# Input projection of a hybrid decoder step, from plain float32 products to three products of rounded parts and rests, with GpSimd making the rests

## The reference, cut to what matters

```
xn = rmsnorm(h, norm1_g)
proj = xn @ w_in + b_in                      # 2048 -> 4096
c_val, c_gate, l_x, l_gate = split(proj)     # 1024 each
u = c_val * sigmoid(c_gate)
c = silu(layernorm(causal_dw_conv(u, width 31)))
lx = causal_dw_conv(l_x, width 4)
r, i = sigmoid(lx @ w_a + b_a), sigmoid(lx @ w_x + b_x)   # per head of 128
log_a = -8 * r * softplus(-lam);  a = exp(log_a)
h_t = a_t * h_{t-1} + sqrt(-expm1(2 log_a)) * i * lx      # over time
h = h + concat(c, hs * gelu(l_gate)) @ w_out
```

## Time and profile before

| what | value |
|---|---|
| median of 3 runs | 1488.46 us (1486.98 to 1491.21) |
| the profiled execution's own time | 1490.41 us |
| its span, first to last instruction | 1488.7 us |
| PE busy | 1383.9 us (93%) |
| DVE busy | 608.9 us (41%) |
| ACT busy | 229.1 us (15%) |
| POOL busy | 40.8 us (3%) |
| mean granted TensorE clock | 0.985 |

### The profile page before, as it was taken

How to read it: one execution, slowest core, us unless ns; L and a number is a source line. 1 busy time by engine, 2 the same in 40 slices (tenths; PEclk the granted TensorE clock), 3 DMA queues, 4 the chain that set the end, 5 groups by cost and what they waited for, 6 DMA issues and landing times.

```text
span 1488.7 us, 19036 instructions
## 1 busy us (share of the span) xinstructions
PE 1383.9 (93%) x7574; PEld 806.0 (54%) x7574; DVE 608.9 (41%) x1030; ACT 229.1 (15%) x369; POOL 40.8 (3%) x56
## 2 busy tenths in 40 slices
PE   8999999999989999999999999989999998997995
PEld 7888888899753333333333333333333333333995
DVE  5689645544542232232223222322232223225764
ACT  2000147533200000000000000000000000003552
POOL 0000000000000000000000000000000000000000
PEclk9999999999999999999999999999999999998998
DMA  9553342345769999999999999999999999999341
GB/s 381 218 198 125 113 122 86 142 142 198 270 241 382 422 422 422 422 422 422 422 422 422 422 422 422 422 421 422 421 422 422 422 422 421 422 422 401 143 142 59
DMA packets 72523, 486.26 MB, mean 327 GB/s; under 512 B 8416, under 2 KB 12544, under 8 KB 15120
## 3 DMA queue, kind: packets, MB, share of 16 engines
q1 hardware_dynamic: 71040, 482.98, 79.8%
q0 software_dynamic: 320, 1.59, 0.3%
q10 hardware_dynamic: 1120, 1.09, 0.2%
HBM read 481.06 MB, written 5.65 MB: 327 GB/s over the span
## 4 chain that ended last, share of the span: by engine, by line
PE 51%; DMA 40%; DVE 3%; ACT 3%; issue 2%; SPq 1%; DVEq 0%; ACTq 0%
DMA ring<-in_w_up_dram 39%; PE ps L816 14%; PE ps L625 14%; PE ps L838 5%; PE ps L688 4%; PE ps L689 4%; PE ps L690 4%; PE ps L849 2%; DVE hT L1551 1%; DMA embedding_rows<-ple_stage 1%; PE ps L634 1%; SPq L472 1%; PE ps L776 1%; PE ps L777 1%; PE ps L715 1%
## 5 line engine op out<-in xcount | busy, mean ns | idle before, releaser
L816 PE MATMUL ps<-ring,xwin 128*64 128x512 f32 x1984 | 452.6, 597 | 37.5 <-DMA ring<-in_w_up_dram 37.2
L1551 DVE TENSOR_TENSOR hT<-hT,ps 128x1056 f32<-128x1056 f32 x128 | 160.4, 1254 | 373.3 <-PE ps L849 372.3
L816 PEld LDWEIGHTS ps<-ring,xwin 128*64 128x64 f32 x1984 | 150.5, 136 | 292.7 <-issue 292.7
L838 PE MATMUL ps<-ring,hid 128*64 128x512 f32 x1024 | 233.6, 610 | 18.8 <-DVE hid L1531 18.8
L625 PE MATMUL ps<-xT,ring 128*128 128x264 f32 x1024 | 229.7, 386 | 0.0
L625 PEld LDWEIGHTS ps<-xT,ring 128*128 128x128 f32 x1024 | 194.5, 190 | 33.5 <-issue 0.3
L838 PEld LDWEIGHTS ps<-ring,hid 128*64 128x64 f32 x1024 | 74.6, 140 | 154.1 <-issue 152.7
L849 PE MATMUL ps<-S,ysb 64*128 64x264 f32 x1024 | 148.3, 408 | 1.3 <-issue 0.8
L849 PEld LDWEIGHTS ps<-S,ysb 64*128 64x128 f32 x1024 | 88.4, 186 | 110.9 <-issue 102.3
L1096 ACT ACTIVATE sgl<-ps 64x512 f32<-64x512 f32 x32 | 18.8, 588 | 575.4 <-PE ps L816 575.4
L1543 DVE COPY ysb<-ps 128x512 f32<-128x512 f32 x32 | 22.1, 691 | 181.8 <-PE ps L838 181.8
(11 more groups left out here) (271 smaller groups left out, 1021.1 us busy)
## 6 DMA issues: line engine op xcount, KB each, us to landing
ring<-in_w_gate_dram SPq DMA_DIRECT2D x128, 1024.0 KB, 23.4
ring<-in_w_up_dram SPq DMA_DIRECT2D x128, 1024.0 KB, 25.4
ring<-in_w_down_dram SPq DMA_DIRECT2D x128, 1024.0 KB, 24.1
ring<-in_w_in_dram SPq DMA_DIRECT2D x32, 1024.0 KB, 7.9
ring<-in_w_out_dram SPq DMA_DIRECT2D x16, 1024.0 KB, 4.8
ring<-in_w_pg_dram SPq DMA_DIRECT2D x16, 1024.0 KB, 5.1
hT<-in_x_dram SPq DMA_DIRECT2D x4, 528.0 KB, 5.2
pleT<-embedding_rows SPq DMA_DIRECT2D x1, 2112.0 KB, 21.5
```

Of the source, the lines that this page charges most:

```text
L816: mm = pe.matmul(ps[part * WIN:(part + 1) * WIN, 0, :], window(k), weights(2 * j + part)[:, kk * F:(kk + 1) * F], start=(k == 0), stop=(k ...
L838: mm = pe.matmul(ps[half * WIN:(half + 1) * WIN, 2 + b, :], hid[:, t, :], weights(8 + t)[:, q * 512:(q + 1) * 512], start=(t == 0), stop=( ...
L1551: dve.tensor_tensor(group(hT, g), group(hT, g), ps[:, bank:bank + 4, 0:TOK].rearrange("p (h k) t -> p h k t", h=2), ALU.add)\
```

## The change

The input projection is now made as the output projection is: weights and xn are rounded, rests are kept, and three float32r products replace each float32 product. Weights come as whole output tiles (48 tiles `t` in one sequence: 32 of `w_in`, 16 of `w_out`), four low slots and four high slots in turn. ACT rounds tile n+3 after it has taken tile n out of PSUM. POOL makes the rests of the first 35 tiles (32 of `w_in`, 3 of `w_out`); DVE makes the others as before. The convolution sums on DVE go to PSUM bank 5 until the last term. `R` has a second buffer, `I2` and `IR` separate two other uses of `I`, and the pieces of the recurrence stand in a new order on PE, ACT and DVE.

```
-CH_IN = 32
...
+W_IN = 32
+W_OUT = 16
+W_FRONT = W_IN + W_OUT
...
+LRU_AT = 23
...
+POOL_RESTS = W_IN + 3
...
     @block.sync
...
-            sp.dma_start(ring[:, slot(n), :], a["w_in"][n]).then_inc(slot_loaded[slot(n)], 16)
...
+        for t in range(PG_SLOTS, W_FRONT):
+            sp.wait_ge(acc_full, t - PG_SLOTS + 1)
             load_tile(t)
+            if t == W_IN + 3:
+                for k in range(CH_PLE):
+                    sp.dma_start(ring[:, PLE_SLOT + k, PLE_HEAD * P:], a["w_ple"][k, :, PLE_HEAD * P:]).then_inc(ple_loaded, 16)
...
+        def rest_weights(t):
+
+            pool.wait_ge(w_hi_ready, t + 1)
...
+            pool.tensor_tensor(lo, ring[:, lo_slot(t), :], hi.bitcast(F32), ALU.subtract).then_inc(w_lo_ready, 1)
+
+        for t in range(POOL_RESTS):
+            rest_weights(t)
...
-        for n in range(CT_OUT):
-            dense(n, 4 * (n // 4), xT, KD, wait_xT if n == 0 else None)
-            if 20 <= n < 28:
-                lru_gates(n - 20)
-            if n == 23:
...
+        hi_hi(0)
+        lo_hi(0, last=False)
+        hi_hi(1)
+        hi_lo(0, last=True)
+        hi_lo(1)
+        lo_hi(1)
+        for n in range(2, W_IN):
+            if n >= 3:
+                pe.wait_ge(acc_free, n - 3 + 1)
+            hi_hi(n)
+            hi_lo(n)
+            if LRU_AT <= n < LRU_AT + 4:
+                lru_gates(2 * (n - LRU_AT))
+            lo_hi(n)
+            if LRU_AT <= n < LRU_AT + 4:
+                lru_gates(2 * (n - LRU_AT) + 1)
+            if n == 22:
                 mean()
-            if 26 <= n < 30:
-                var(n - 26)
+            if n == 26:
+                var()
...
+        for k in range(KD):
+            act.wait_ge(xT_ready, k + 1)
+            act.activation(x_part(k), xT[:, k, :], ACT.Copy).then_inc(x_hi_ready, 1)
...
+            round_weights(n + 3)
+            if n == 24:
+                betas(0)
...
+        for k in range(KD):
+            dve.wait_ge(x_hi_ready, k + 1)
+            dve.tensor_tensor(x_lo[:, k, :], xT[:, k, :], x_part(k).bitcast(F32), ALU.subtract).then_inc(x_lo_ready, 1)
...
+                    part = ps[:, 5, j % 2 * SEQ:j % 2 * SEQ + SEQ]
...
-                        last[j] = step(stt(mix[:, j, 0:SEQ], U[:, j, t:t + SEQ], w, mix[:, j, 0:SEQ],
+                        last[j] = step(stt(mix[:, j, 0:SEQ] if t == CK - 1 else part, U[:, j, t:t + SEQ], w, part,
```

More of the change, by code:

```diff
@@ L40 @@
 PG_SLOTS = 4
[L41 to L48, removed]
+EXP_SLOT = [8, 0, 9, 1, 10, 2, 11, 3, 4, 5, 6, 7]
+HEAD_SLOT = 4
+MIX_SLOT = 4
+X_SLOT = 6
+PLE_SLOT = 6
+MIX_ORDER = list(range(KD))
+LRU_AT = 23
+TAIL_LO = [8, 9, 10, 11, 4, 6]
+TAIL_HI = [0, 1, 2, 3, 5, 7]
 TAIL_SLOTS = len(TAIL_LO)
@@ L599, in turn, with embed @@
             return pe.matmul(out, src, ident[:, :], start=True, stop=True)
[L601 to L627, removed]
+        def embed(n):
+            pe.wait_ge(ple_taken, n - 3 - CT_PLE + 1) if n - 3 >= CT_PLE else pe.wait_ge(h1_ready, n - 3 - CT_OUT + 1)
+            if n == CT_PLE:
+                pe.wait_ge(ple_loaded, 32)
+            m = PLE_HEAD + n - CT_PLE
+            for k in range(CH_PLE):
+                mm = pe.matmul(ps[:, n % 3, 0:TOK], ring[:, PLE_SLOT + k, m * P:(m + 1) * P], pT[:, k, :],
+                               start=(k == 0), stop=(k == CH_PLE - 1))
             mm.then_inc(acc_full, 1)
         pe.wait_ge(consts_ready, 5)
[L631 to L634, removed]
+        for q in range(XQ):
+            pe.wait_ge(x_summed, q + 1)
+            mm = pe.matmul(ps[:, 0, 0:TOK], ones[:, :], T[:, q, :], start=(q == 0), stop=(q == XQ - 1))
         mm.then_inc(row_full, 1)
@@ L660, in mean, with var @@
             mm.then_inc(mean_full, 1)
-        def var(p):
-            pe.wait_ge(sq_ready, 2 * p + 2)
-            for j in range(2 * p, 2 * p + 2):
-                mm = pe.matmul(ps[:, 7, 0:TOK], ones[:, :], sq[:, j % 2, :], start=(j == 0), stop=(j == TC - 1))
+        def var():
+            pe.wait_ge(sq_ready, 2)
+            for j in range(TC):
+                mm = pe.matmul(ps[:, 7, 0:TOK], ones[:, :], sq[:, j, :], start=(j == 0), stop=(j == TC - 1))
             mm.then_inc(sq_used, 1)
-        def wait_xT(k):
-            pe.wait_ge(xT_ready, k + 1)
@@ new lines, in lo_hi @@
+        def lo_hi(n, last=True):
+            pe.wait_ge(*rest_in(n))
+            for k in range(KD):
+                mm = pe.matmul(ps[:, n % 3, 0:TOK], ring_r[:, lo_slot(n), k, :], x_part(k), start=False,
+                               stop=(last and k == KD - 1))
+            if last:
+                mm.then_inc(acc_full, 1)
+        hi_hi(0)
[15 more added lines that the diff above has]
+            if n == 22:
@@ L1046, in _ @@
                     round_mix(j)
-        act.wait_ge(mixr_ready, TC)
-        round_mix(KD - 1)
-        round_weights(2)
+            if n == 30:
+                for j in range(6):
+                    act.wait_ge(mixr_ready, j + 1)
+                    round_mix(TC + j)
+        for j in (6, 7):
+            act.wait_ge(mixr_ready, j + 1)
+            round_mix(TC + j)
         def square_h1(m):
```

388 lines of the change are left out of this document (208 added, 180 removed).

## The result

The changed kernel takes 1516.12 us in the median of 4 runs (1515.13 to 1517.12), the kernel before 1489.84 in the 4 runs beside them: a ratio of 1.0177, with an interval from 1.0155 to 1.0199. It is slower by 26 us where the forecast had 1470.9 and a range up to 1500. The profiled execution has a span of 1514.8 us against 1488.7 before; the first output tile ("the mark") ends at 296.5 and not at 271.2, 25 us later, so the loss lies ahead of it and is carried nearly unchanged to the end.

The account below looks back on a forecast made before the run. PE was taken to bound the input stage, up to the first output tile's end at 271.2 us. Gain 27.6 less 10 for collisions is 17.6, off 1490.41: 1472.8, or 1470.9 on the median's footing; range 1455 to 1500.

Parts of the forecast that it names:

- Tile 1: Start of the input stage: its end taken at 35.5 us against 33.5 before, a loss of 2 us.
- stall at tile 25: Second pair of gate products in tile 25: PE waits 7 us for PSUM banks that ACT's gates clear.
- that at tile 26: PE waits 2 us more for ACT at tile 26, until 200.5 us.
- Without collisions: End of the first output tile if no DVE instruction meets a POOL subtraction: 243.6 us, a gain of 27.6.
- the step on collisions: Behind tile 22, DVE instructions with two SBUF inputs meet POOL subtractions: 0 to 17 us together, taken as 10.
- four places: Both halves of the second recurrence, the scaling by the deviation, the last rests of mix: 0 to 4.2 us each.
- a collision or so in each group: Convolution on DVE, four groups from 47.7 us: ends at 156 instead of 150, still in time for the mean.
- this sign of being wrong: Listed under what would show the forecast wrong: waits of the mean on the convolution.
- Strict turns: Rival, chance 0.18: whole subtractions alternate with single two-input DVE instructions; gain only 6 us, time 1482.5.
- The other slower rivals: POOL's subtraction as dear as its select, 1509 us, chance 0.09; sums in PSUM exposing their chain, 1496.9, chance 0.06.
- the exposed chain: Rival, chance 0.06: convolution sums in PSUM add 28 us on DVE, 2 find room; time 1496.9.
- POOL at its dearest: Rival, chance 0.09: a POOL subtraction takes 7.95 us like its select; first output tile 21 us slower, time 1509.

Follow-up runs that it names:

- e2_memset: The changed kernel with GpSimd writing zeros instead of subtracting, so the rests of those weights are left out: 1461.5 us in one run.
- e5_conv: The changed kernel with small operations and gates of the convolution freed of second SBUF operands, and state products made by POOL: 1484.8 us.
- e6_tail: The changed kernel with POOL's last six tiles of rests (29 to 34) made by DVE instead: 1497.1 us.
- e1_small: The changed kernel with the kc operations at the start of DVE's program and the spt scratch in PSUM: 1514.0 us.
- e8_nodma: The changed kernel with GpSimd's two DMA issues after its fifth subtraction moved to the SyncE queue: 1516.4 us.

## Why the prediction was wrong, point by point

*Right.* Tile 1 ended at 36.1 (forecast 35.5). The tiles of the input stage follow at 5.83 us (5.84). POOL's subtraction takes 4.7 us (4.2, within its bounds), under the pace of a tile, so PE waited only 3.5 us in six places for rests of weights. The Trainium skill (GPSIMD Engine Reference, Performance versus the Vector engine) gives 4.5 us for a two-input operation of this size; a subtraction undisturbed took 4.50, the mean of 35 with the disturbed ones 4.71. The sums in PSUM cost nothing more. The stall at tile 25 on ACT's gates was 7.5 us (7), that at tile 26 1.4 (2). Without collisions the mark would be at 243.8 (243.6): shown by e2_memset.

*Wrong: the step on collisions.* The prediction wrote "on the chain behind tile 22 four places can meet a subtraction ... each costs 0 to 4.2, together 0 to 17; I take 10". The loss against the mark without collisions is 52.7 us (296.5 less 243.8). It failed in three ways.

First, it looked behind tile 22 only. Ahead of it, it had the convolution start "when tile 3 is out, at 47.7", and gave it "a collision or so in each group". The chain between the rests of x and the first tap, nineteen instructions of DVE of which thirteen are 128x1 or 128x8 and take some 0.2 us each, was not in the working at all. It cost 28 us of start, and 9.3 us more were lost between the third and the fourth group; a slack of 16 us took part of it, and 21.5 us reached the mean. e5_conv gives 31.3 us back when these alone are cured. The prediction had named this sign of being wrong itself: waits of the mean on the convolution.

Second, the tail. Six places and not four met a subtraction (a product of the recurrence, the sum of 128x32, a gate's product, one of the scalings, two rests of mix), and the upper end of one collision was a whole subtraction, right in kind; a gate's product met a subtraction and a DMA issue (6.3 us), and the rests of mix met two in a row (9.2). PE waited 17.3 us there against 2.0 in e2_memset. e6_tail gives 19.0 us back, where the forecast took 10 and 17 as the upper end.

Third, the feedback. The gates' buffer is free when DVE has multiplied with it, so while DVE waits for POOL, ACT waits for DVE and rounds nothing. The timeline of ACT:

```profile
75.90 0.48 ACT L1055 ACTIVATE sg<-ps,vT 128x264 f32<-128x264 f32 x1 [14.16 <-DVE U L1313]
```

After those 14.2 us it rounds one tile after the other, and POOL has four subtractions in a row from 78.25 on, and again beside each later group; the last such row reached from 129 to 161 us and met DVE between the third and the fourth group. In e5_conv, where the first tap stands at 49.1, ACT no longer waits for DVE there, and from 68 to 166 us POOL's subtractions come one at a time, 5.83 us apart. The prediction had ACT, POOL and DVE each within the pace of a tile and took that for enough.

*The rival that had it.* "Strict turns" named the mechanism: a subtraction is held whole and meets one DVE instruction after the other. Its price, 22 us of loss, was less than half of the 52.7, since it counted turns at nearly the same places. It had a chance of 0.18 and deserved more: the one row that showed a collision fits a wait for the end of the other engine's whole instruction. Its strict alternation did not always hold: one product waited through four subtractions. The other slower rivals were wrong: POOL was not as dear as its select, and the sums in PSUM exposed no chain.

*The range* ended at 1500, past the exposed chain (1496.9), and left out POOL at its dearest (1509). The chain ahead of the first tap had no price in it and the tail too low a one; with both the time is 1516.

## What to carry to other kernels

Before a GpSimd instruction of microseconds is put beside DVE's work, list every DVE operation on a chain that reads two operands from SBUF (or is a tensor-scalar one from SBUF to SBUF), the smallest too, and price each at one whole GpSimd instruction: it is the count that costs, not the size. The cure has to take the whole chain: one operand of each in PSUM, or the work given to GpSimd itself, or GpSimd's share ended ahead of it; taking a part only moved the wait (e1_small). With it the change pays, 1465.2 us with all of its arithmetic.

## What the runs showed of the hardware that was not expected

An operation of 128x1 that takes 0.16 us alone (e2_memset) took 4.35 us, to the end of a subtraction that ran. One that came while GpSimd issued a DMA waited 19.0 us, through four subtractions that followed each other without a pause; with the issues moved away (e8_nodma) eight operations waited for one each instead. With subtractions of a quarter the length, operations of 128x8 waited 11.7 to 22.5 us, through 9 to 18 of them, with no DMA issue near. In turn a run of DVE operations with two SBUF inputs holds GpSimd off: its second subtraction, beside the rests of x, took 7.6 us and not 4.5. None of this was seen for operations with one operand in PSUM, 232 of them 0.39 us apart, and a reciprocal of 128x8, which reads one operand, took its 0.20 us beside a running subtraction (e8_nodma).
